# Half of a mixture-of-experts gate table summed in HBM by indirect DMAs, the other half by one-hot products among 56 expert inputs

## Chip, core and metric

The kernel runs on one core of one Trainium2 chip. Its metric is the device time of one execution in microseconds; less is better.

## What is computed

Two transformer-like blocks over 256 tokens of width 1024, in f32. The change is in the last part, a retrieval from 128 x 128 = 16,384 experts ("PEER"). Cut to what matters:

```python
q = (x @ peer_w_q).reshape(n_tok, 8, 2, 128)            # 8 heads, two halves
s = einsum('thcd,hckd->thck', q, sub_keys)              # scores of 2 x 128 sub-keys
v_top, i_top = lax.top_k(s, 16)
cand = v_top[:, :, 0, :, None] + v_top[:, :, 1, None, :]
best, pos = lax.top_k(cand, 16)                         # 16 of 256 pairs, for each head
expert = i_top_0 * 128 + i_top_1                        # at pos
gate = softmax(best)
act = gelu(einsum('tkd,td->tk', u_emb[expert], x)) * gate
out = einsum('tk,tkd->td', act, v_emb[expert])          # 8 x 16 experts a token
```

## The kernel before, in words

The kernel does not gather experts. It computes the inputs u.x of all 16,384 experts for all tokens, multiplies them by a dense gate table, and sums the outputs. Experts are taken in 128 groups of 128: group e holds the experts whose second sub-key is e, with the first sub-key on the partitions. So the work of group e is one **input** product ("up": 128 experts x 256 tokens, over 8 tiles of the width), a Gelu on ScalarE, three operations on VectorE that multiply by the gates and split the result into a high and a low part (`gate`), and one **output** product ("down": 256 tokens x 1024, over the 128 experts, accumulated in four PSUM banks until the end).

**Weights.** SyncE streams pages of 1 MB (two pieces of 128 x 1024) from `in_stream` into a ring of three. A page is sent when the pieces of the page three before it have been taken. A piece is used in one of two ways: *whole* (f32, straight from the ring; `whole`), or *split*: ScalarE writes its high part to one of three `piece` buffers (`high`, line 1217), VectorE the low part (`low`, line 1730), and PE makes three products of high and low parts (`fm_piece`, `down`). ScalarE may write a piece when PE has begun the piece two before it.

**Selection.** VectorE finds the best pairs head by head (`select`). For each head it makes a one-hot of the places in the lists (line 2381), GpSimd numbers them (`number`, lines 425 and 431), and one head later VectorE sums the result into `selv` (`gather`, line 2389; the last head's in line 2472): row number, column number and gate of each token's 128 experts.

**The gate table.** `selv` is transposed (line 1116), so that for each token the 128 chosen experts lie on the partitions. Then for each token VectorE (line 2483, and line 2480 for four tokens at a time) and ScalarE (lines 1655 and 1661, every other four tokens) write a one-hot of the row numbers and a one-hot of the column numbers times the gates; PE multiplies the two (a product of 128 x 128 x 128), and ScalarE copies four tokens at a time to the table `G` (line 1646), which takes the whole arena, 128 KB of each partition.

**Order.** The query products, then nine whole inputs under the selection, the transposes, a tenth input, the 256 tokens of one-hot products with the whole inputs 10 to 13 put between them, step by step, one split input (14), 13 outputs, then rounds of one output and one input (113 of them, groups of six in a loop), two outputs, and the final norm. The inputs that run ahead are kept in `early`, 15 tiles of 128 x 256.

**Other places that the change touches.** In the FFN of the first block GpSimd does two multiplications for each of 22 page turns (`gated_page`, lines 389 and 392). Between 50 and 157 us it issues 16 plain DMAs of 1 MB (line 370) for modulation weights. `acc_free`, `acc_ready`, `a_ready`, `lo_ready`, `piece_used` are semaphores, named for what they count. `SCRATCH` is the memory for GpSimd's DMA descriptors. All matrix products are recorded at line 462 (the transposes of `selv` at 1116).

Of the kernel before, what the change touches and what calls it, by code (L numbers as in the profile page):

```python
# [14 lines left out]
P = 128  # L15
D = 1024
KD = D // P
L = 256
RING = 3
LOOP = 6  # L20
EARLY = 15
CHOICE = 10
SCRATCH = 1024
F32 = mybir.dt.float32
# [10 lines left out]
         ("gt", 8), ("pm", 2), ("pr", 2), ("w2", 4), ("wq", 8), ("early", EARLY // 2), ("first", (EARLY - 1) // 2),  # L35
         ("peer", 129 - EARLY)]
# [10 lines left out]
NWHOLE = PAGE["first"] - WHOLE0  # L47
# [13 lines left out]
for _name, _n in TURNS:  # L61
# [7 lines left out]
        ("if_b", 2), ("eps6", 1), ("eps_gn", 1), ("eps_ml", 1)]  # L69
# [14 lines left out]
def widths(table):  # L84
# [14 lines left out]
 p1_mm mt_ready places place_no placed hi_ready g_mm selt_sb piece_used acc_ready hn_mm hn_sq hn_sqmm  # L99
# [3 lines left out]
 p1_sb x_mm xa_mm lv_sb u0_mm xa_sb s_sb sa_mm sa_sb ds_mm u0_sb y_mm y_sb xs_root x_in_psum subk_in key_sb  # L103
 key_mm selt_ready selt_mm oh_ready row_hot g_sb a_ready experts_done ach hn_cs hn_ln hn_root xfin c_in cols_in
 lg_ready root1 hraw h_hi wctx_arg wctx w_q part_hi decay_arg conv_mid conv_u mqk_conv lf_abs lf_ln mqk_taps
 m_arg m_exp zs_ready kk_root scan_done g_arg g_exp row_square fg_in fin_sq fin_root dch h_new part_in up_chain
# [3 lines left out]
def build(nc, t, out):  # L110
    with ExitStack() as ctx:
# [13 lines left out]
        early = place("early", SPARE, [EARLY, L])  # L125
# [36 lines left out]
        def pair(name, hi, lo, a):  # L162
# [110 lines left out]
        eqb = at(19456, 2048)  # L273
        selv = at(21504, 768).rearrange("p (t c n) -> p t c n", t=2, c=3)
        gsm = at(22272, 64)
        subk = at(28672, 2048).rearrange("p (g n) -> p g n", g=16)
        G = arena[:, 0:32768].rearrange("p (n e) -> p n e", e=128)
        selT = at(0, 768, late).rearrange("p (c n) -> p c n", c=3)

        row_hot = [v.rearrange("p (n e) -> p n e", n=4) for v in (at(768, 512, late), at(1280, 512, late), row_more, small)]  # L280
        up_bank = (TURN["peer"] + EARLY - 1) % 2
        gate_banks = (6, 7, 1 - up_bank)
        col_hot = [v.rearrange("p (n e) -> p n e", n=2) for v in (at(1792, 256, late), cols[:, 0:256],
                                                                  pc[:, 0:256])]
        col_hot = [[v[:, 0], v[:, 1]] for v in col_hot] + [[cols[:, 256:384], pc[:, 256:384]]]
        gelu_t = at(0, 512, late).rearrange("p (b n) -> p b n", b=2)
        a_r = late_r[:, 768:1792].rearrange("p (c b n) -> p c b n", c=2, b=2)
# [29 lines left out]
        def _(sp):  # L317
# [35 lines left out]
            pages_split(PAGE["first"] + RING, NPAGES - PAGE["first"] - RING, 2 * (WHOLE0 - SPLIT0))  # L353


# [9 lines left out]
        def _(pool):  # L365
# [27 lines left out]

            with pool.Fori(0, 3) as i:
                for u in range(LOOP):
                    gated_page(u, i)
            for u in range(18, 22):
                gated_page(u)
# [35 lines left out]
            for hh in range(7):  # L434
                number(hh)

            first = PAGE["first"]
            for s in range(2):
                c = piece_no(first) + s
                if s == 0:  # L440
                    pool.wait_ge(loaded[first % RING], 16 * (first // RING + 1))
                pool.wait_ge(S["piece_used"], c - 1 - s)
                g.tensor_copy(piece[:, 0, c % 3], ring[:, first % RING, s]).then_inc(S["hi_ready"], 1)
# [3 lines left out]
        def _(pe):  # L447
# [25 lines left out]
            def turn(T, i=0):  # L473

                v = T // 2 + LOOP // 2 * i
                if not (isinstance(v, int) and v <= 0):
                    pe.wait_ge(acc_free[T % 2], v)
# [624 lines left out]
            m.then_inc(S["x_in_psum"], 1)  # L1102
# [5 lines left out]

            for e in range(CHOICE - 1):
                early_up(e)  # L1110
            pe.wait_ge(S["key_sb"], 8)
            for tt in range(2):
                pe.wait_ge(S["selt_ready"], tt + 1)
                pe.wait_ge(S["placed"], 8)
                for c in range(3):
                    m = nc.tensor.transpose(ps[:, 6 + tt, c * P:(c + 1) * P], selv[:, tt, c, :], ident)
                m.then_inc(S["selt_mm"], 1)
            early_up(CHOICE - 1)


            def scatter(q):
                for b in range(2):
                    pe.wait_ge(S["oh_ready"], 2 * q + b + 1)
                    if b == 0:
                        if q % 2 == 1:
                            pe.wait_ge(S["row_hot"], q // 2 + 1)
                        if q >= 3:
                            pe.wait_ge(S["g_sb"], q - 2)
                    for e in range(2):
                        c = 2 * b + e  # L1130
                        m = mm(ps[:, gate_banks[q % 3], c * P:(c + 1) * P], row_hot[q % 4][:, c, :],
                               col_hot[2 * (q % 2) + b][e], start=True, stop=True)
                    m.then_inc(S["g_mm"], 1)

            def early_step(n):
                e, k = CHOICE + n // 8, n % 8
                T, p = TURN["peer"] + e, PAGE["early"] + e // 2
                if k == 0:
                    turn(T)
                    turn(T + 1)  # L1140
# [1542 lines left out]
```

## Time and profile before

| | us |
|---|---|
| device time, median of 3 runs | 1698.72 (1697.33 to 1699.45) |
| profiled execution, span | 1701.3 (its device time is not given apart from the span) |
| PE busy in it | 1646.9 (97%) |
| VectorE, ScalarE, GpSimd busy | 1174.0, 801.9, 99.0 |
| DMA | 278.94 MB, mean 164 GB/s |

The profile is of one more execution. In it, L462 is line 462 of the kernel; PE is TensorE's matmul, PEld its weight load, DVE VectorE, ACT ScalarE, POOL GpSimd, SP SyncE; a q behind an engine's name is its instruction queue. An f32 product leaves two records, a product of split parts one. Matmuls overlap, and their ends are modelled: a group's length is a little more than the time to the start of the next, so steps are best read from starts.

### The profile page before, as it was taken

Reading aid. Unit: us, or ns where it says so; the run is one execution under the profiler, and the core shown is the slowest. Engines: PE = TensorE matmul, PEld = TensorE weight load, DVE = VectorE, ACT = ScalarE, POOL = GpSimd, SP = SyncE. Lnnn points to the kernel's source line nnn. Section 1 sums busy time; section 2 is a strip of 40 time slices with the busy share of each in tenths; the row PEclk is TensorE's granted clock in tenths of the full one; section 3 lists DMA queues with packets and bytes.
Section 4 is the critical chain, followed back from the end, with each engine's and each line's share of the span. In section 5 each row is a group of like instructions: output and inputs, shape, how many; then the busy total and the mean of one; then the engine's idle time right before and its main releaser. Section 6 shows DMA issues by size and latency. Waiting matters only on the chain.

```text
span 1701.3 us, 32624 instructions
## 1 busy us (share of the span) xinstructions
PE 1646.9 (97%) x12606; PEld 1510.4 (89%) x12606; DVE 1174.0 (69%) x2143; ACT 801.9 (47%) x1223; POOL 99.0 (6%) x124
## 2 busy tenths in 40 slices
PE   8999999999999999989999989999999999999998
PEld 3999978999999998879898878999999999999997
DVE  3756656777846769647498998666666666666665
ACT  2423436566634675425213993444444444444444
POOL 0000000022200001110052000000000000000000
PEclk9999999999999999999999999999999999999999
DMA  8876414545554433204333015555555555455553
GB/s 307 303 272 223 149 50 149 189 175 191 179 176 149 152 144 125 101 4 158 115 124 124 26 50 187 185 195 176 196 178 192 185 185 193 177 197 176 194 183 126
DMA packets 38826, 278.94 MB, mean 164 GB/s; under 512 B 4432, under 2 KB 4560, under 8 KB 5328
## 3 DMA queue, kind: packets, MB, share of 16 engines
q1 hardware_dynamic: 35424, 254.82, 42.1%
q0 software_dynamic: 2304, 16.78, 2.6%
q10 hardware_dynamic: 1008, 6.05, 0.9%
q8 instruction: 68, 1.11, 0.3%
q14 instruction: 22, 0.18, 0.0%
HBM read 276.58 MB, written 1.05 MB: 163 GB/s over the span
## 4 chain that ended last, share of the span: by engine, by line
PE 86%; DVE 7%; ACT 4%; issue 2%; DMA 1%; DVEq 0%; POOL 0%; SPq 0%; ACTq 0%; POOLq 0%
PE ps L462 86%; DVE piece L1730 2%; DMA ring<-in_stream 1%; ACT piece L1217 1%; DVE pconst_sb L2483 1%; DVE cols L2483 0%; DMA arena<-in_xT 0%; DVE late L2483 0%; DVE arena L1780 0%; ACT arena L1256 0%; DVE arena L1833 0%; DVEq L2483 0%; ACT arena L1575 0%; ACT L1252 0%; DVE arena L1797 0%
## 5 line engine op out<-in xcount | busy, mean ns | idle before, releaser
L462 PEld LDWEIGHTS ps<-h_r,piece 128*128 128x128 f32 x5664 | 699.2, 192 | 19.8 <-issue 8.7
L462 PE MATMUL ps<-h_r,piece 128*128 128x256 f32 x5664 | 708.4, 284 | 4.6 <-DVE piece L1730 3.7
L1730 DVE TENSOR_TENSOR piece<-ring,piece 128x1024 fp32r<-128x1024 f32 x434 | 533.2, 1237 | 241.7 <-ACT piece L1217 240.3
L1217 ACT ACTIVATE piece<-ring 128x1024 fp32r<-128x1024 f32 x432 | 452.6, 1056 | 356.8 <-PE ps L462 352.7
L462 PE MATMUL ps<-piece,late_r 128*128 128x512 f32 x1536 | 370.1, 391 | 1.4 <-DVE late_r L2505 1.4
L462 PEld LDWEIGHTS ps<-piece,late_r 128*128 128x128 f32 x1536 | 281.1, 188 | 55.3 <-issue 1.8
L2500 DVE TENSOR_TENSOR late<-late,arena 128x256 f32<-128x256 f32 x113 | 72.0, 638 | 117.6 <-ACT late L1686 117.6
L1686 ACT ACTIVATE late<-ps 128x256 f32<-128x256 f32 x113 | 43.5, 385 | 200.5 <-PE ps L462 200.5
L462 PE MATMUL ps<-arena,ring 128*128 128x256 f32 x480 | 110.5, 379 | 1.6 <-DVE arena L1797 1.6
L462 PEld LDWEIGHTS ps<-arena,ring 128*128 128x128 f32 x480 | 88.1, 190 | 12.3 <-issue 2.0
L462 PE MATMUL ps<-arena 64*64 64x64 f32 (+7 forms) x930 | 87.4, 297 | 7.6 <-DVE arena L2266 1.8
L462 PEld LDWEIGHTS ps<-arena 64*64 64x64 f32 (+4 forms) x930 | 68.6, 162 | 22.1 <-issue 10.4
L1244 ACT ACTIVATE arena<-ps 128x512 f32<-128x512 f32 x43 | 25.6, 595 | 97.0 <-PE ps L462 97.0
L462 PE MATMUL ps<-ffn_hi,piece 128*128 128x256 f32 x352 | 63.5, 283 | 1.2 <-DVE piece L1730 1.2
L2505 DVE TENSOR_TENSOR late_r<-late,late_r 128x256 fp32r<-128x256 f32 x128 | 54.5, 426 | 4.4
L462 PEld LDWEIGHTS ps<-ffn_hi,piece 128*128 128x128 f32 x352 | 54.9, 192 | 1.4 <-DVE piece L1730 1.4
L462 PE MATMUL ps<-ffn_lo,piece 128*128 128x256 f32 x176 | 49.8, 283 | 0.0
L462 PE MATMUL ps<-mg_hi,piece 128*128 128x256 f32 x256 | 42.8, 284 | 0.5 <-DVE arena L1995 0.5
L2503 DVE CAST late_r<-late 128x256 fp32r<-128x256 f32 x128 | 37.7, 294 | 4.4
L462 PE MATMUL ps<-piece,h_r 128*128 128x256 f32 x288 | 38.9, 297 | 0.0
L462 PEld LDWEIGHTS ps<-mg_hi,piece 128*128 128x128 f32 x256 | 37.7, 192 | 0.9 <-DVE arena L1995 0.9
L462 PEld LDWEIGHTS ps<-piece,h_r 128*128 128x128 f32 x288 | 37.8, 205 | 0.8 <-issue 0.8
(325 smaller groups left out, 1709.5 us busy)
## 6 DMA issues: line engine op xcount, KB each, us to landing
ring<-in_stream SPq DMA_DIRECT2D x240, 1024.0 KB, 4.8
arena<-in_mod POOLq DMA_DIRECT2D x16, 1024.0 KB, 6.2
arena<-in_const ACTq DMA_DIRECT2D x1, 2256.0 KB, 10.6
arena<-in_const ACTq DMA_DIRECT2D x1, 1648.0 KB, 8.8
xres<-in_xT SPq DMA_DIRECT2D x1, 1024.0 KB, 5.3
arena<-in_xT SPq DMA_DIRECT2D x1, 1024.0 KB, 7.1
arena<-in_subk ACTq DMA_DIRECT2D x1, 1024.0 KB, 4.9
out<-arena SPq DMA_DIRECT2D x4, 256.0 KB, 2.1
```

What stands on the lines that cost most here:

```text
L462: mm_last[0] = nc.tensor.matmul(*args, **kw)
L1217: A(piece[:, 0, c % 3], ring[:, p % RING, s], ACT.Copy).then_inc(S["hi_ready"], 1)
L1244: A(dst, ps[:, T % 2, src], func, **kw).then_inc(acc_free[T % 2], 1)
L1686: A(gelu_t[:, e % 2, :], ps[:, T % 2, 0:L], ACT.Gelu).then_inc(acc_free[T % 2], 1)
L1730: TT(piece[:, 1, c % 3], ring[:, p % RING, s], piece[:, 0, c % 3].bitcast(F32), ALU.subtract).then_inc(S["lo_ready"], 1)
L2483: ins = TS(col_hot[b % 4][e], iota, selT[:, 1, bass.ds(16 * i + (2 * b + e), 1)], selT[:, 2, bass.ds(16 * i + (2 * b + e), 1)], ALU.is_equ ...
L2500: TT(a_t, ready, G[:, :, bass.ds(LOOP * i + e, 1)].rearrange("p n a -> p (n a)"), ALU.mult).then_inc(S["a_chain"], 1)
L2503: V.tensor_copy(a_r[:, 0, b, :], a_t).then_inc(S["a_chain"], 1)
L2505: TT(a_r[:, 1, b, :], a_t, a_r[:, 0, b, :].bitcast(F32), ALU.subtract).then_inc(S["a_ready"], 1)
```

## The change

Tokens 0 to 127 and tokens 128 to 255 get their gates in different ways.

- **Tokens 0 to 127**: the table is an HBM tensor `gate_table` of 128 x 128 x 128. GpSimd writes zeros to it with eight DMAs of 1 MB, issued during the FFN (from a tile `zero`). As each head is selected, VectorE works out its gates (`gate_arg` to `gate_end`, with one small Exp of ScalarE for each head, `gate_exp`) and its positions `gidx` (expert x 128 + token). GpSimd adds each of the 16 columns of a head to the table with an indirect DMA (one element for each of 128 tokens, `compute_op=add`): four after each numbering of heads 1 to 6, the other 104 after it. Before the first DMA of a head it waits for those of the head before. SyncE waits for all 128, then fetches the table back, two expert groups at a time, into three tiles `gtile`, between the pages.
- **Tokens 128 to 255**: one transposition, one-hots on VectorE alone, and one-hot products in groups of four tokens (`quad`) behind two of each three split inputs. The table `G` for them takes 64 KB of each partition, laid out with tokens innermost.
- **Order**: 16 whole inputs, 2 split inputs, three transposes, 54 split inputs with 32 groups of four tokens among them, 56 rounds of one output and one input, 72 outputs. So 72 inputs run ahead of the first output; they are kept in the arena and in `early` (now 12 tiles). The pages of the stream are in that order.
- **Gates** are now two multiplications of 128 x 128, one from `gtile` and one from `G`, then the cast and the subtraction as before, in a ring of three buffers instead of two.

```diff
-EARLY = 15
-CHOICE = 10
-SCRATCH = 1024
+CHUNK = 4
+EARLY = 16
+AHEAD = 72
+SCRATCH = 4096
...
+            for p in range(UPS + RING, PEER + 2):
+                next_page(p)
+            sp.wait_ge(S["scat"], 2048)
+            for m in range(RING):
+                gate_in(m)
+            m = RING
+            for n in range(2, P - AHEAD // 2):
+                next_page(PEER + n)
+                if n > P - AHEAD or (n < P - AHEAD and n >= 2 * m - 1):
+                    gate_in(m)
+                    m += 1
...
+            def gate_in(m):
+
+                if m >= RING:
+                    sp.wait_ge(S["a_ready"], 2 * (m - RING) + 2)
+                sp.dma_start(gtile[:, m % RING], gate_pair[m]).then_inc(g_in[m % RING], 16)
...
+            g.memset(zero, 0.0).then_inc(S["mqk_pad"], 1)
...
                     gated_page(u, i)
+                    if u % 3 == 0:
+                        pool.dma_start(gate_zero[u // 3 + 2 * i], zero).then_inc(S["zeroed"], 16)
+            for n in range(6, 8):
+                pool.dma_start(gate_zero[n], zero).then_inc(S["zeroed"], 16)
...
+            def scatter(first, last):
+                for n in range(first, last):
+                    hh, k = n // 16, n % 16
+                    if k == 0:
+                        pool.wait_ge(S["gate_at"], 2 * hh + 2)
+                        if hh:
+                            pool.wait_ge(S["scat"], 256 * hh)
+                    g.indirect_dma_start(gtab[:, :], bass.IndirectOffsetOnAxis(ap=gidx[:, hh, k:k + 1], axis=0),
+                                         gw[:, hh, k:k + 1], None, compute_op=ALU.add).then_inc(S["scat"], 16)
+
+            number(0)
+            for hh in range(1, 7):
                 number(hh)
+                scatter(CHUNK * (hh - 1), CHUNK * hh)
+            scatter(6 * CHUNK, 128)
...
+            def quad(q, i=0):
+                pe.wait_ge(S["oh_ready"], q + 1 + 8 * i)
+                if not isinstance(i, int) or q >= 2:
+                    pe.wait_ge(S["g_sb"], q + 8 * i)
+                for n in range(4):
+                    m = mm(ps[:, 6 + q % 2, n * P:(n + 1) * P], row_hot[q % 2][:, n, :], col_hot[q % 2][:, n, :], start=True,
+                           stop=True)
+                m.then_inc(S["g_mm"], 1)
...
+            with pe.Fori(1, 4) as i:
+                for n in range(2 * LOOP):
+                    up(EARLY + 8 + n, C0 + 8 + n, i)
+                    if n % 3 < 2:
+                        quad(2 * (n // 3) + n % 3, i)
+            def both(k, i=0):
+                down(k, C1 + 2 * k, i)
+                up(AHEAD + k, C1 + 2 * k + 1, i)
...
+            for e in range(EARLY - 2):
+                gelu(e)
+                if e in (1, 4, 7, 11):
+                    gate_exp(4 + (1, 4, 7, 11).index(e))
...
+                if n >= 8 and (n - 8) % 3 < 2:
+                    q = 2 * ((n - 8) // 3) + (n - 8) % 3
+                    act.wait_ge(S["g_mm"], q + 2)
+                    A(G[:, :, 4 * q:4 * q + 4].rearrange("p e n -> p n e"),
+                      ps[:, 6 + q % 2, :].rearrange("p (n e) -> p n e", n=4), ACT.Copy).then_inc(S["g_sb"], 1)
...
+            def gate_end(hh):
+
+                after(roots[hh])
+                for tt in range(2):
+                    ins = TT((gw[:, hh], wsel(hh)[:, 1])[tt], wsel(hh)[:, tt],
+                             gsm[:, 2 * hh + tt:2 * hh + tt + 1].to_broadcast([P, 16]), ALU.mult)
+                ins.then_inc(S["gate_at"], 1)
+                after(nos[hh])
+                TS(gidx[:, hh, :], no_t, 128.0, col("tok"), ALU.mult, ALU.add).then_inc(S["gate_at"], 1)
...
+            def onehots(q):
+                r, c = row_hot[q % 2], col_hot[q % 2]
+                if q >= 2:
+                    dve.wait_ge(S["g_mm"], q)
+                TT(r, iota.unsqueeze(1).to_broadcast([P, 4, P]),
+                   selT[:, 0, 4 * q:4 * q + 4].unsqueeze(2).to_broadcast([P, 4, P]), ALU.is_equal)
+                for n in range(4):
+                    ins = TS(c[:, n, :], iota, selT[:, 1, 4 * q + n:4 * q + n + 1], selT[:, 2, 4 * q + n:4 * q + n + 1],
+                             ALU.is_equal, ALU.mult)
+                ins.then_inc(S["oh_ready"], 1)
...
+            def gate(e):
+                m, b = e // 2, e % 3
+                z, a_t = gtile[:, m % RING, e % 2, :], z_of(e)
+                if e % 2 == 0:
+                    dve.wait_ge(g_in[m % RING], 16 * (m // RING + 1))
+                if e >= 3:
+                    d = e - 2
+                    dve.wait_ge(S["piece_used"], piece_no(PEER) + (2 * d if d < P - AHEAD else P - AHEAD + d) + 1)
+                elif e == 0:
+                    dve.wait_ge(S["g_sb"], 33)
+                    dve.wait_ge(acc_free[(TURN["peer"] + AHEAD - 1) % 2], (TURN["peer"] + AHEAD - 1) // 2 + 1)
+                TT(a_t[:, 0:P], a_t[:, 0:P], z, ALU.mult).then_inc(S["a_chain"], 1)
+                TT(a_t[:, P:L], a_t[:, P:L], G[:, e, :], ALU.mult).then_inc(S["a_chain"], 1)
...
+            for k in range(P - AHEAD):
+                low(PEER + k, 0)
+                gate(k)
+                low(PEER + k, 1)
+            for n in range(P - AHEAD, P - AHEAD // 2):
+                for s in range(2):
+                    low(PEER + n, s)
+                    gate(2 * n - (P - AHEAD) + s)
```

## Rows read from the trace of the kernel before

**Rows 1.** The page, chain of work that ended last: share of the span by engine.

```profile
PE 86%; DVE 7%; ACT 4%; issue 2%; DMA 1%; DVEq 0%; POOL 0%; SPq 0%; ACTq 0%; POOLq 0%
```

**Rows 2.** Stretches: from:to, length, busy us (instructions) of each engine, PEclk, DMA share, GB/s.

```profile
921.00:1014.00 93.00, 80.99 (x595) 73.60 (x596) 88.88 (x290) 88.47 (x230) 2.02 (x2) 1.00 0.10 35
1057.00:1690.00 633.00, 632.84 (x4058) 577.64 (x4058) 420.72 (x563) 271.08 (x338) 0.00 (x0) 1.00 0.52 184
```

**Rows 3.** Timeline of PE: start, length, line, tiles, number of records, [idle before].

```profile
888.52 31.25 PE L462 MATMUL ps<-arena,ring 128*128 128x256 f32 x144
920.98 0.85 PE L1116 MATMUL ps<-pconst_sb,arena 128*128 128x128 f32 x6 [1.22 <-DVE arena L2472]
...
925.95 0.68 PE L462 MATMUL ps<-late 128*128 128x128 f32 x4 [0.68 <-ACT early L1244]
...
934.95 0.61 PE L462 MATMUL ps<-late,row_more 128*128 128x128 f32 x4
...
935.85 0.60 PE L462 MATMUL ps<-arena,ring 128*128 128x256 f32 x2
...
1014.35 3.11 PE L462 MATMUL ps<-h_r,piece 128*128 128x256 f32 x24
...
1021.58 35.62 PE L462 MATMUL ps<-piece,late_r 128*128 128x512 f32 x156 [1.38 <-DVE late_r L2505]
1057.37 3.14 PE L462 MATMUL ps<-h_r,piece 128*128 128x256 f32 x24 [0.16 <-DVE piece L1730]
...
1689.79 5.63 PE L462 MATMUL ps<-piece,late_r 128*128 128x512 f32 x24
```

**Rows 4.** Timeline of ScalarE and VectorE behind one input of the loop.

```profile
1060.63 0.39 ACT L1686 ACTIVATE late<-ps 128x256 f32<-128x256 f32 x1 [1.78 <-PE ps L462]
1060.91 1.05 ACT L1217 ACTIVATE piece<-ring 128x1024 fp32r<-128x1024 f32 x1
1061.17 0.63 DVE L2500 TENSOR_TENSOR late<-late,arena 128x256 f32<-128x256 f32 x1 [1.06 <-ACT late L1686]
...
1062.17 0.43 DVE L2505 TENSOR_TENSOR late_r<-late,late_r 128x256 fp32r<-128x256 f32 x1
```

**Rows 5.** Timeline of VectorE in the one-hot stretch.

```profile
936.18 0.68 DVE L2480 TENSOR_TENSOR late<-pconst_sb,late 128x512 f32<-128x512 f32 x1
936.78 0.60 DVE L2483 TENSOR_SCALAR late<-pconst_sb,late 128x128 f32<-128x128 f32 x2
```

**Rows 6.** Timeline of VectorE in the selection of the last two heads.

```profile
904.20 1.23 DVE L2381 TENSOR_TENSOR arena<-pconst_sb,arena 128x1024 f32<-128x1024 f32 x1
...
911.91 0.26 DVE L2389 TENSOR_TENSOR arena<-arena 128x64 f32<-128x64 f32 x1
...
913.75 1.23 DVE L2381 TENSOR_TENSOR arena<-pconst_sb,arena 128x1024 f32<-128x1024 f32 x1
```

**Rows 7.** Timeline of ScalarE, between two early Gelus.

```profile
916.75 1.28 ACT L1634 ACT_TABLE_LOAD   x1
```

**Rows 8.** The stretch in which GpSimd's plain DMAs run; columns as in rows 2.

```profile
50.00:160.00 110.00, 109.14 (x922) 108.46 (x922) 74.21 (x68) 41.87 (x60) 8.66 (x16) 0.98 0.76 284
```

**Rows 9.** Timeline of all engines where GpSimd issues one of them.

```profile
75.07 1.22 DVE L1730 TENSOR_TENSOR piece<-ring,piece 128x1024 fp32r<-128x1024 f32 x1
...
75.45 0.53 POOL L370 DMA_DIRECT2D arena<-in_mod  x1 [1.93 <-DVE arena L1885]
```

**Rows 10.** DMA issues: number, KB each, median us from issue to landing.

```profile
ring<-in_stream SPq DMA_DIRECT2D x240, 1024.0 KB, 4.8
...
out<-arena SPq DMA_DIRECT2D x4, 256.0 KB, 2.1
```

**Rows 11.** Timeline of GpSimd: the end of the last numbering.

```profile
908.08 2.68 POOL L431 TENSOR_TENSOR arena<-arena 128x512 f32<-128x512 f32 x3
```

**Rows 12.** Timeline of GpSimd and VectorE, where GpSimd casts.

```profile
930.49 2.02 POOL L443 CAST piece<-ring 128x1024 fp32r<-128x1024 f32 x2 [19.73 <-DMA ring<-in_stream]
930.53 2.06 DVE L2483 TENSOR_SCALAR cols<-pconst_sb,late 128x128 f32<-128x128 f32 x2
```

More of the change, by code:

```diff
@@ L280, in build @@
[L280 to L285, printed above, removed]
@@ L1118, in _ @@
[L1118 to L1133, printed above, removed]
@@ L1199, in _ @@
+            C2 = C1 + P - AHEAD
+            with pe.Fori(0, 5) as i:
+                for e in range(P - AHEAD, P - AHEAD + 2 * LOOP):
+                    down(e, C2 + e, i, 2 * LOOP)
+            for e in range(P - AHEAD + 10 * LOOP, P):
+                down(e, C2 + e)
         @block.scalar
@@ L1624, in _ @@
                     key_evac(u - 1)
+                if u in (3, 4, 6, 7):
+                    gate_exp((3, 4, 6, 7).index(u))
             key_evac(7)
[L1627 to L1634 removed]
@@ L1692, in _, with gelu @@
-            split(PAGE["peer"])
-            rounds = (P - EARLY) // LOOP
-            with act.Fori(0, rounds) as i:
-                for u in range(LOOP):
-                    split(PAGE["peer"] + 1 + u, i)
-                    gelu(EARLY + u, i)
-            for u in range(LOOP * rounds, P - EARLY):
-                split(PAGE["peer"] + 1 + u)
-                gelu(EARLY + u)
+            def gelu(e):
+                if e >= AHEAD:
+                    act.wait_ge(S["a_ready"], e - AHEAD + 1)
+                evac(TURN["peer"] + e, z_of(e), ACT.Gelu, slice(0, L))
@@ L1701, in _ @@
+            for k in range(P - AHEAD):
+                split(PEER + 1 + k)
+                gelu(AHEAD + k)
+            for n in range(P - AHEAD + 1, P - AHEAD // 2):
+                split(PEER + n)
             act.wait_ge(S["a_ready"], P)
@@ L2512, in _ @@
-            for e in range(EARLY - 2):
-                early_gate(e)
-                if e < EARLY - 3:
-                    low(PAGE["first"] + (e + 2) // 2, (e + 2) % 2)
-            low(PAGE["peer"], 0)
-            early_gate(EARLY - 2)
-            early_gate(EARLY - 1)
-            low(PAGE["peer"], 1)
-            rounds = (P - EARLY) // LOOP
-            with dve.Fori(0, rounds) as i:
-                for u in range(LOOP):
-                    split(PAGE["peer"] + 1 + u, i)
-                    gate(EARLY + u, i, gelu_t[:, (EARLY + u) % 2, :])
@@ L2525, in _ @@
-            for u in range(LOOP * rounds, P - EARLY):
-                split(PAGE["peer"] + 1 + u)
-                gate(EARLY + u, 0, gelu_t[:, (EARLY + u) % 2, :])
+            for k in range(P - AHEAD):
+                low(PEER + k, 0)
[5 more added lines that the diff above has]
+                    gate(2 * n - (P - AHEAD) + s)
             dve.wait_ge(S["fg_in"], 16)
```

304 lines of the change are left out of this document (125 added, 179 removed).

## Prediction

> **What bounds the kernel now.** I read the page first: PE is busy for most of the span, and 86% of the chain that ended last is its matmuls [rows 1]. Since a busy PE need not be at its best rate, the second view is the table of stretches around the change [rows 2]. The reader is to see two kinds there: the one-hot stretch (921 to 1014), where VectorE and ScalarE are busier than PE and DMA all but rests at 35 GB/s, and the expert rounds (from 1057), where PE has no free time in 633 us and VectorE has a third of it. The third view is PE's timeline, which gives the step of each kind of product by the starts of neighbouring groups [rows 3]:
> - a whole f32 expert input: nine (144 records) take 31.25 us: 3.47.
> - one expert output ("down"): 13 lie between 1021.58 and 1057.37: 35.79 / 13 = 2.753 us.
> - one output and one split input: 113 rounds lie between 1054.62 (1057.37 less one output) and 1689.79: 5.621 us. So a split input takes 2.868 us.
> - one token's one-hot product: four tokens between 934.95 and 935.85: 0.225 us each.
> - the end: the last two outputs start at 1689.79 and end in step at 1695.3; 6.0 us of final norm follow.
>
> The one-hot stretch from 925.95 to 1014.35 lasts 88.4 us: 256 x 0.225 = 57.6 us of one-hot products, 4 x 3.47 = 13.9 us of expert inputs put between them, and 16.9 us of waits for one-hot rows. That, with the waits beside it, is what can be gained; everything else in the expert phase is products that stay.
>
> **The sum, along PE's queue.** Nothing before 888.5 is on it (below). From there:
> - 16 whole inputs (before: 14): 55.5, to 944.0.
> - 56 split inputs: 160.6. Three transposes instead of six (which took 0.85 at 920.98): 0.4. 128 tokens of one-hot products: 28.8. To 1133.8.
> - The first output waits: gate(0) now waits for the evacuation of input 71, the last before it. In the loop of before the input ends in step at 1060.24, ScalarE's Gelu runs from 1060.63 to 1061.02, VectorE's chain from 1061.17 to 1062.60 [rows 4]. The strided multiply (0.63) gives way to two contiguous ones over half as many elements, 0.2 each, so the chain is 1.2: 0.4 + 0.4 + 0.15 + 1.2 = 2.2 us, to 1136.0.
> - 56 rounds of output and input: 314.8. 72 outputs: 198.2. Tail 6.0. End: 1655.0.
>
> That is 46.3 us under the profiled span of 1701.3, which is 2.6 us above the median of the runs shown. The forecast is 1698.7 - 46.3 = 1652 us. From the other side: gone are 128 tokens (28.8), the waits of the stretch (16.9) and around it (1.22 at 920.98, 0.68 at 925.95, 0.16 at 1057.37, and 1.5 at 1021.58, which starts 7.23 us after 1014.35 where an input and an output take 5.62), and 0.4 of transposes; added are the slower form of two inputs (1.2) and the new wait (2.2): -46.3.
>
> **What has to stay hidden.** *VectorE and ScalarE in the 56 inputs.* Three inputs and two groups of four tokens take PE 3 x 2.868 + 2 x 0.90 = 10.4 us. VectorE then does three low parts (1.22 each [rows 9]) and two sets of one-hots: a row multiply (step 0.60) and four comparisons (0.60 for two, 0.34 for one: step 0.26) [rows 5], 3.7 + 3.3 = 7.0 us. ScalarE does three high parts (1.05), three Gelus (0.39) [rows 4] and two evacuations of twice a Gelu's elements (0.6, or 1.2 if the strided write doubles it): 5.6 to 6.8 us. Both fit. If each of the 32 groups still caught PE out by the 0.16 us of 1057.37, that is +5; I take none.
> *VectorE in the 72 outputs alone.* The 13 outputs before 1057 are this pattern (low part, multiply, cast, subtraction), and PE doesn't wait among them. The multiply gets cheaper; the tiles' arrival is rival 3.
> *Selection on VectorE.* Seven small operations a head (0.1 to 0.2 each), less those for all heads at the end: some 5 us. The places of the last head are summed at 926 instead of at 920.98 less a little [rows 3]. PE asks for them only after 18 inputs, at 949.7, and for the first low part at 944.0. Each of the last four Exp costs ScalarE a table load before it and one after it (1.28 [rows 7]); with a Gelu that is some 3.2 us inside a step of 3.47. Head 7's values are found near 918 (911.9 now [rows 6]), ScalarE comes to its Exp at 930. Nothing on the path.
> *GpSimd's zeroing.* Eight writes of 1 MB each during the FFN, one to three pages of 5.74 us (two split inputs' products each). Nearest row: between 50 and 160 us 16 DMAs of GpSimd run beside the stream at 284 GB/s, and PE is busy for 109.1 of 110 us [rows 8]. A page that lands in 4.8 us [rows 10] has some 9 us from issue to use (two pages less 2.5 for its parts). I take 0; 8 x 1 us would be the cost if that cover were short.
>
> **The indirect DMAs, the unknown price.** GpSimd issues 128, each for 128 single elements; call its time for one X. Below: 0.53 us, a plain DMA of 128 rows from GpSimd [rows 9]. Above: 2.1 us, the landing of the one kind of DMA into HBM here [rows 10], as if each ran alone. It must read an index for each row and add to HBM, so it lies off the lower end, but nothing makes it wait for a landing within a head: I take 1.3. 24 are issued between heads, four after each numbering. Numbering ends at 910.76 [rows 11], 5.3 us after VectorE's one-hot of the places (904.20 to 905.4), and is wanted at 911.9, with 9.55 us from head to head [rows 6]. Four at 1.3 are 5.2 us; free are 9.55 - 5.3 + 0.7 (the new operations) + 1.1 = 6.1, so selection isn't held up. The other 104 start at 915 and, with six waits for a head's landing at 2.1, end at 915 + 104 X + 12.6: at 983, 1063 or 1146 for X = 0.53, 1.3, 2.1. SyncE waits for them, with the pages of expert pair 2 and after, and VectorE's first gate tile, queued behind: due at about 1128. At my value 65 us are left.
>
> **Rivals.**
> *1. The table is late.* From X = 1.93 each further 0.1 us costs 10.4 us; at X = 2.37 the gain is gone. At the upper bound of 2.1 the time is 1670. Against it: a plain issue takes a quarter of that. For it: no row shows an adding DMA of single elements, and if the DMA engines take each addition as a round trip, X is theirs, not GpSimd's.
> *2. GpSimd locks VectorE out: slower.* At 930.49 GpSimd runs two casts in 2.02 us; the two comparisons that VectorE starts at 930.53 take 2.06 together instead of 0.60: one comparison gets through per GpSimd instruction [rows 12]. If an indirect DMA does the same, then per three inputs VectorE needs 3.7 + 1.2 + 8 x (0.34 + X) = 18.0 us at X = 1.3 where PE needs 10.4, for as long as the scattering lasts. It also stretches selection (up to four waits in each of six heads, 31 us: PE stands still from 944 for 14), so the last 104 start at 947; some 79 are left at the first one-hots, 12 go per three inputs: 6.6 x 7.6 = 50 us. The time is 1652 + 14 + 50 = 1716. It decides against the change from X = 1.15 on; at X = 1.0 the same sum gives 1689. Against it: at 75.45 GpSimd issues a plain DMA amid VectorE's low part, and that takes 1.22 us, the DMA 0.53, as each does alone [rows 9]. But that is a subtraction of two operands; no row has a comparison or a cast beside a DMA issue.
> The Trainium skill (SBUF — State Buffer, "Who interferes with whom") says that GpSimd and a VectorE scalar operation or copy in its two-port mode take one shared pair of ports as an exclusive lock for the whole instruction, and that generating descriptors needs that pair. The casts beside the comparisons agree; by the whole rule this rival, and not the forecast, would hold.
> *3. Gate tiles hold up the stream.* In the 72 outputs SyncE waits for a gate before it sends the next tile, the next page behind it. If page and tile went one after the other (4.8 + 2.1 us [rows 10]), two outputs would take 6.9 instead of 5.5: 36 x 1.4 = 50 us, no change. Against it: three pages are in flight, and the traffic, 1.18 MB in 5.5 us or 214 GB/s, is under the 284 of [rows 8].
>
> **How the numbers follow.** Forecast 0.70. Rival 1 0.11, of which 0.05 still faster (1655 to 1695) and 0.06 slower. Rival 2 0.14: 0.06 in part or with a short X (1655 to 1690), 0.08 slower. Rival 3 0.03, the same. Others 0.02. Faster 0.81, the same 0.04, slower 0.15, where 0.2% is about what a measurement can tell from no change. The forecast's own range is 1647 (all of the new wait and of the two inputs' 1.2 hidden, one-hots 2 us cheaper in bulk) to 1660 (+5 at the groups, +3 of zeroing). With the faster halves of rivals 1 and 2 the range is 1642 to 1690.
>
> **What would show it.** Right: split inputs from about 944, the first output at about 1136, outputs alone from about 1451, PE without idle time in each; comparisons at 0.34; GpSimd's last indirect DMA well before 1128. Wrong: comparisons of 1 us and more with PE waiting for them (rival 2); a gap of PE at 1136 released by a DMA, with SyncE waiting for the scatter (rival 1); PE waiting for pages or tiles after 1451 (rival 3). What makes the forecast wrong is above all X over 1.93, or a lock with X over 1.15.

## The result and the profile after

| | before | after |
|---|---|---|
| median | 1699.1 us (4 runs, 1697.3 to 1700.1) | 1709.3 us (4 runs, 1706.4 to 1711.8) |
| span of the profiled execution | 1701.3 us | 1710.1 us |
| ratio of the times | | 1.0059, 95% interval 1.0043 to 1.0074 |

The change makes the kernel slower by 0.6%. 1652 was forecast.

The first view to read is the table of stretches: the one in which inputs and one-hot products run together, and the one after it (columns as in rows 2).

```profile
1000.00:1100.00 100.00, 79.28 (x629) 76.44 (x628) 48.52 (x91) 42.93 (x58) 71.54 (x42) 0.98 0.47 114
1210.00:1504.00 294.00, 294.00 (x1884) 268.19 (x1883) 185.93 (x313) 125.72 (x158) 0.00 (x0) 1.00 0.56 198
```

In the rounds PE is busy for 294.00 of 294.00 us, as before [rows 2]. Amid the one-hots it is busy for 79 of 100, and there no other engine is full: VectorE has 49, ScalarE 43, GpSimd 72. So nobody lacks capacity; somebody waits in the wrong order. PE's timeline shows where (start, length, line, tiles, number of records, [idle before]):

```profile
886.90 55.42 PE L512 MATMUL ps<-arena,ring 128*128 128x256 f32 x256
941.97 6.10 PE L512 MATMUL ps<-h_r,piece 128*128 128x256 f32 x48
...
1140.72 1.16 PE L512 MATMUL ps<-late 128*128 128x128 f32 x8 [1.58 <-DVE late L2507]
1141.63 3.11 PE L512 MATMUL ps<-h_r,piece 128*128 128x256 f32 x24
1146.03 1.16 PE L512 MATMUL ps<-row_more,late 128*128 128x128 f32 x8 [1.28 <-DVE row_more L2507]
1146.94 5.99 PE L512 MATMUL ps<-h_r,piece 128*128 128x256 f32 x48
1154.22 1.16 PE L512 MATMUL ps<-late 128*128 128x128 f32 x8 [1.28 <-DVE late L2507]
...
1193.44 2.97 PE L512 MATMUL ps<-piece,late_r 128*128 128x512 f32 x12 [1.98 <-DVE late_r L2537]
```

The whole inputs take the 55 us of the sum, and the split inputs start at 941.97 where 944 was said. The reader is then to see the brackets: every group of four tokens (x8) finds PE idle for 1.3 us and more, until VectorE's comparisons (L2507) are done. Three inputs and two groups take 1154.22 - 1140.72 = 13.5 us where the sum had 10.4. The first output starts at 1193.44, 57.4 us behind the 1136.0 of the sum. From there to the end of the span are 516.7 us; the sum had 519.0. All of the error lies between 942 and 1193.

What VectorE and ScalarE did around one such group, in their timelines, with PE's in the same stretch:

```profile
1055.25 1.16 PE L512 MATMUL ps<-late 128*128 128x128 f32 x8 [1.43 <-DVE late L2507]
1056.17 3.10 PE L512 MATMUL ps<-h_r,piece 128*128 128x256 f32 x24
1060.56 1.16 PE L512 MATMUL ps<-row_more,late 128*128 128x128 f32 x8 [1.29 <-DVE row_more L2507]
```

```profile
1056.57 1.06 ACT L1249 ACTIVATE piece<-ring 128x1024 fp32r<-128x1024 f32 x1 [4.26 <-PE ps L512]
1057.53 0.36 ACT L1276 ACTIVATE arena<-ps 128x256 f32<-128x256 f32 x1
1057.79 1.11 ACT L1688 ACTIVATE arena<-ps 128x512 f32<-128x512 f32 x1
```

```profile
1057.66 1.22 DVE L1724 TENSOR_TENSOR piece<-ring,piece 128x1024 fp32r<-128x1024 f32 x1 [2.46 <-ACT piece L1249]
1058.80 0.68 DVE L2504 TENSOR_TENSOR late<-pconst_sb,late 128x512 f32<-128x512 f32 x1
1059.40 1.11 DVE L2507 TENSOR_SCALAR row_more<-pconst_sb,late 128x128 f32<-128x128 f32 x4
```

This is a ring of waits. PE begins an input at 1056.17; only then is a slot in the ring of three pieces free, and ScalarE makes the high part of the input two further on (1056.57 to 1057.63). VectorE waited 2.46 us for it, since that input's low part stands in its queue ahead of the one-hots (low part to 1058.88, one-hots to 1060.51). PE, done with its input, waits for these one-hots at 1060.56. From the start of an input to the one-hots behind it pass 4.39 us of other engines' serial work, though PE needs 2.87; the difference comes back at every group. The one-hots themselves had all their data the whole time.

The second view is the source line of the indirect DMAs (times in ns min/median/max; first and last start), and the source line of the comparisons.

```profile
L486 POOL DMA_INDIRECT gate_table<-early x128: 1548/1561/2601, 862.4 to 1183.7; - x128
its engine sat idle before it (us, times) until:
  issue: 69.1, 123
  DMA gate_table<-early: 11.2, 5
```

```profile
L2507 DVE TENSOR_SCALAR late<-pconst_sb,late x64: 333/342/659, 968.8 to 1183.3; 128x128 f32<-128x128 f32 x64
L2507 DVE TENSOR_SCALAR row_more<-pconst_sb,late x64: 335/340/559, 974.1 to 1184.9; 128x128 f32<-128x128 f32 x64
...
  PE ps L512: 46.5, 31
```

A comparison takes 0.34 us with indirect DMAs beside it most of the time, as it does alone [rows 5]. The median indirect DMA takes 1.56 us, with 0.30 before the next: 1.86, above the 1.3 taken. The last one starts at 1183.7; in the sum it was issued by 1063. Around the first output:

```profile
1187.35 1.41 SPq L379 DMA_DIRECT2D early<-gate_table  x3
...
1191.50 0.38 ACT L1276 ACTIVATE early<-ps 128x256 f32<-128x256 f32 x1 [0.43 <-PE ps L512]
1192.01 0.29 DVE L2532 TENSOR_TENSOR arena<-arena,early 128x128 f32<-128x128 f32 x1 [3.93 <-ACT early L1276]
```

The gate tiles are asked for at 1187.35, and VectorE's first gate multiply still waits for the Gelu, not for them. So the table came just in time, for a first output that was 57 us late for another reason. Each of the two delays, that of the inputs (57 us) and that of the table (due at about 1128, asked for at 1187), is longer than the 46 us that were to be gained, and the profile shows only the one that ended last.

### The profile page after: what moved, and what is told of

Same layout as the page of the kernel before. It is cut to its first block, busy times and chain, and to the rows that moved or that the text cites. A ratio compares the mean times of both kernels' runs of the same rounds, so it can differ in the third digit from the quotient of the medians.

```text
span 1710.1 us, 30322 instructions
## 1 busy us (share of the span) xinstructions
PE 1625.2 (95%) x12331; PEld 1489.3 (87%) x12331; DVE 1129.1 (66%) x2190; ACT 754.0 (44%) x1042; POOL 319.9 (19%) x259
## 4 chain that ended last, share of the span: by engine, by line
PE 80%; DVE 10%; ACT 5%; DMA 2%; issue 2%; DVEq 0%; POOL 0%; SPq 0%; POOLq 0%
PE ps L512 80%; DVE piece L1724 4%; ACT piece L1249 3%; DVE late L2504 1%; DVE late L2507 1%; DVE row_more L2507 1%; DMA ring<-in_stream 1%; DMA arena<-in_const 1%; DMA arena<-in_xT 0%; DVE arena L1774 0%; ACT arena L1288 0%; DVE arena L1827 0%; ACT arena L1607 0%; ACT L1284 0%; DVE arena L1791 0%
## 5 line engine op out<-in xcount | busy, mean ns | idle before, releaser
L512 PEld LDWEIGHTS ps<-h_r,piece 128*128 128x128 f32 x5616 | 692.6, 193 | 15.3 <-issue 9.2
L512 PE MATMUL ps<-piece,late_r 128*128 128x512 f32 x1536 | 359.0, 390 | 2.0 <-DVE late_r L2537 2.0
L486 POOL DMA_INDIRECT gate_table<-early x128 | 217.0, 1695 | 80.2 <-issue 69.1
L1276 ACT ACTIVATE arena<-ps 128x256 f32<-128x256 f32 (+1 forms) x163 | 71.3, 437 | 256.6 <-PE ps L512 256.6
L512 PEld LDWEIGHTS ps<-arena,ring 128*128 128x128 f32 x512 | 96.7, 190 | 14.8 <-issue 2.0
L512 PEld LDWEIGHTS ps<-arena 64*64 64x64 f32 (+4 forms) x930 | 70.3, 169 | 22.0 <-issue 10.4
L426 POOL TENSOR_TENSOR arena<-arena 128x256 f32<-128x256 f32 x22 | 16.2, 737 | 211.4 <-DVE arena L2049 211.4
L2537 DVE TENSOR_TENSOR late_r<-arena,late_r 128x256 fp32r<-128x256 f32 x120 | 51.1, 426 | 4.1
L1688 ACT ACTIVATE arena<-ps 128x512 f32<-128x512 f32 x32 | 35.2, 1101 | 33.0 <-PE ps L512 30.9
L512 PE MATMUL ps<-row_more,late 128*128 128x128 f32 x128 | 18.9, 291 | 24.7 <-DVE row_more L2507 24.7
L470 POOL TENSOR_TENSOR arena<-arena 128x512 f32<-128x512 f32 x14 | 20.4, 1686 | 116.3 <-DVE arena L2375 116.3
```

The costliest lines, as they stand in the source:

```text
L426: g.tensor_tensor(v, ga[:, b, :], v, ALU.mult).then_inc(S["gated"], 1)
L470: g.tensor_tensor(e[:, 2 * c:2 * c + 2], e[:, 2 * c:2 * c + 2], topf[:, :, 2 * hh + c, :].unsqueeze(2).to_broadcast([P, 2, 16, 16]), ALU.m ...
L486: g.indirect_dma_start(gtab[:, :], bass.IndirectOffsetOnAxis(ap=gidx[:, hh, k:k + 1], axis=0), gw[:, hh, k:k + 1], None, compute_op=ALU.ad ...
L512: mm_last[0] = nc.tensor.matmul(*args, **kw)
L1276: A(dst, ps[:, T % 2, src], func, **kw).then_inc(acc_free[T % 2], 1)
L1688: A(G[:, :, 4 * q:4 * q + 4].rearrange("p e n -> p n e"), ps[:, 6 + q % 2, :].rearrange("p (n e) -> p n e", n=4), ACT.Copy).then_inc(S["g_ ...
```

## The experiments

**1. One-hots one input earlier.** VectorE's queue alone is changed:

```diff
-            for n in range(NU + 2):
+            for n in range(NU + 1):
                 if n < NU:
                     low(UPS + n // 2, n % 2)
-                p = n - 2
+                p = n - 1
```

> The changed kernel with one edit: VectorE makes the one-hots for the group behind input p after the low part of piece p+1 instead of p+2. Theory A (VectorE's queue order: the low part of piece p+2 can't start before PE has begun input p, and the one-hots stand behind it): PE's 46.5 us of waits for one-hots nearly all go (under 5 us left) and the split inputs end near 1145 instead of 1191. But GpSimd's last indirect DMA still ends near 1185, so the first output still starts at about 1193 and the time stays within 5 us of 1709: the wait moves to the table. Theory B (GpSimd's DMA issue locks VectorE's comparisons out, my rival 2): the waits for one-hots stay above 35 us.

Measured: 1723.1 us, ratio 1.0136 (1.0116 to 1.0156). PE's timeline of this kernel:

```profile
1124.55 3.11 PE L512 MATMUL ps<-h_r,piece 128*128 128x256 f32 x24
1203.57 4.68 PE L512 MATMUL ps<-piece,late_r 128*128 128x512 f32 x12 [75.91 <-DVE late_r L2537]
```

No group waits any more and the inputs end at 1127.7. The order was the cause of the 46.5 us. But PE then stands still for 75.9 us, until the table is there: the wait has moved, and grown. The time is 14 us above the changed kernel's, where at most 5 were expected. The last indirect DMA starts at 1197.0, 13 us later than in the changed kernel, though the 25th started 5 us sooner: long DMAs cost 9.5 us more and gaps over 0.6 us 8.5 us more.

**2. and 3. No indirect DMAs**, in the changed kernel and in the one of experiment 1 (both leave out the gates of tokens 0 to 127):

```diff
-                    g.indirect_dma_start(gtab[:, :], ..., gw[:, hh, k:k + 1], None, compute_op=ALU.add).then_inc(S["scat"], 16)
+                    g.engine_nop().then_inc(S["scat"], 16)
```

> The changed kernel without the 128 indirect DMAs (the gates of tokens 0 to 127 stay zero, the semaphore is counted up by empty instructions), the order of VectorE as it is. Theory A: the waits for one-hots stay (over 35 us), since they have nothing to do with GpSimd; selection ends some 10 us earlier, off the path; time 1700 to 1710. Theory B: the waits go, time about 1655.

> Both edits: one-hots one input earlier, and no indirect DMAs (gates of tokens 0 to 127 stay zero). Theory A: PE runs through the split inputs, first output near 1137, time 1652 to 1660, the sum of the prediction. Theory B gives the same; what would speak against both is a time above 1670.

Measured: 1708.6 us (ratio 1.0063, 1.0040 to 1.0086) with the one-hots where the change has them, 1651.0 us (ratio 0.9716, 0.9699 to 0.9733) with the one-hots early. Without a single indirect DMA the groups' waits are the same 46.4 us (24.7 + 21.7), so GpSimd has no part in them. With both obstacles away the sum of the prediction holds to a microsecond:

```profile
1125.28 1.06 PE L511 MATMUL ps<-late 128*128 128x128 f32 x8
...
1129.04 1.06 PE L511 MATMUL ps<-row_more,late 128*128 128x128 f32 x8
1129.86 3.11 PE L511 MATMUL ps<-h_r,piece 128*128 128x256 f32 x24
1134.95 2.99 PE L511 MATMUL ps<-piece,late_r 128*128 128x512 f32 x12 [1.98 <-DVE late_r L2536]
```

The four corners (1709.3, 1723.1, 1708.6, 1651.0) are to be read together: taking away either cause alone gives nothing or loses 14 us, taking away both gives 58.

**4. A quarter of the room for descriptors:** `SCRATCH = 1024` in the changed kernel, the value of before.

> The changed kernel with a quarter of the memory for GpSimd's DMA descriptors (1024 instead of 4096). GpSimd stands idle for 45 us in 16 gaps of 1.7 to 6 us between indirect DMAs. If it waits there for room for descriptors, the gaps get longer and more (over 80 us), and the last DMA ends after 1220, time over 1740. If the gaps have another cause (a fetch of instructions, a wait for the DMA engines that carry pages), they stay at 35 to 55 us and the time at 1709.

Measured: 1802.2 us (one run); over 1740 was expected if the gaps are waits for room.

```profile
L486 POOL DMA_INDIRECT gate_table<-early x128: 1548/1565/2498, 865.2 to 1275.1; - x128
its engine sat idle before it (us, times) until:
  issue: 153.6, 122
```

The DMAs themselves are as short as before, but the idle time ahead of them grows from 69.1 to 153.6 us, in gaps of 1.7 to 5.7 us after one to three DMAs. Part of the gaps is a wait for room. Counting the DMAs shows which: with 1,024 bytes the gaps over 1.6 us stand behind each 3rd and each 7th DMA, and with 4,096 bytes, in the changed kernel, behind each 15th and each 28th. Some are hidden by a numbering or by the wait at a head's end.

**5. Half the rows in each indirect DMA**, one-hots early: `gidx[0:64, ...]`, `gw[0:64, ...]`. The gates of tokens 64 to 127 are left out.

> One-hots one input earlier, and each indirect DMA takes the gates of tokens 0 to 63 alone (64 rows in place of 128; the gates of tokens 64 to 127 are left out). Theory A (the price of an indirect DMA goes with its rows, and so does the room that its descriptors take): one takes about 0.8 us in place of 1.56, no gaps beside the waits between heads, the table is done before the last input ahead, the first output's product starts near 1135 and the time is that of the kernel without scatter, 1651, within 4 us. Theory B (a fixed price for each DMA): one still takes about 1.56 us and 1.86 with its gap, only the gaps for room go: last DMA at about 928 + 104 x 1.86 + 11 (between heads) = 1132 to 1150, first output near 1140 to 1158, time 1657 to 1675.

Measured: 1681.2 us (ratio 0.9901, 0.9873 to 0.9929), above both ranges.

```profile
L486 POOL DMA_INDIRECT gate_table<-early x128: 1408/1416/3066, 859.7 to 1154.3; - x128
```

Half the rows take 1.416 us in place of 1.56: a straight line through the two gives an estimate of some 1.27 us fixed and 2.3 ns for each row. Theory A falls. The gaps over 0.6 us sum to 34 us against 53 in experiment 1, so those for room don't all go, as theory B had it, and the table is late by 31.2 us of PE's time. The gaps now stand behind each 28th and each 51st DMA: one count goes by rows (15 to 51), the other doesn't.

**6. to 8. Room, with a control.** One-hots early; 68 inputs ahead in place of 72, and three buffers of earlier stages elsewhere, leave 8,192 bytes. The control is the same kernel with 4,096; the third has `CHUNK = 5`.

```diff
-AHEAD = 72
-SCRATCH = 4096
+AHEAD = 68
+SCRATCH = 8192
```

> One-hots one input earlier, 8,192 bytes of descriptor room in place of 4,096; the room comes from 68 expert inputs ahead in place of 72 (the table is then due 11.5 us earlier) and from buffers of an earlier stage put elsewhere. Nothing is left out. Theory A (the gaps that are not at a head's end are waits for room): some 34 us of gaps go, the last indirect DMA is issued at 928 + 104 x 1.86 + 11 (between heads) + 0 to 17 (lengthened ones) = 1132 to 1150, first output near 1157 against 1124 due, time 1651 + 33 = 1684 (1672 to 1694), so below the kernel before. Theory B (the gaps come from the DMA engines being shared with the weights and stay whatever the room): last DMA near 1190, time 1651 + 75 = 1726 or more.

> The same kernel as the one with 8,192 bytes of room, with 4,096 again (68 ahead, all else the same): the control. Both theories: the last indirect DMA as late as with one-hots early and 72 ahead, 1197, first output near 1203, and as the inputs end 11.5 us earlier the wait is 87 us and the time 1723 + 11 = 1734 (1726 to 1740).

> 8,192 bytes of room, one-hots early, 68 ahead, and five indirect DMAs behind each head's numbering in place of four, so that 98 in place of 104 are left behind the last. Theory A (GpSimd has that much time between the heads: 6.2 us of numbering and 5 x 1.86 = 15.5 us against a period of 12.6, so it hasn't): the heads' period grows toward 15.5 and the selection becomes later, the time is 0 to 20 us above that of four. Theory B (selection has slack before TensorE needs it): 6 DMAs earlier, 11 us less than with four.

Measured: 1725.7 (ratio 1.0153, 1.0129 to 1.0178), 1732.0 (1.0196, 1.0158 to 1.0234) and 1721.8 us (1.0123, 1.0097 to 1.0149). First 8,192, then 4,096 bytes:

```profile
L486 POOL DMA_INDIRECT gate_table<-early x128: 1548/1557/3037, 861.3 to 1185.9; - x128
its engine sat idle before it (us, times) until:
  issue: 53.5, 123
```

```profile
L486 POOL DMA_INDIRECT gate_table<-early x128: 1547/1559/3318, 860.2 to 1193.3; - x128
its engine sat idle before it (us, times) until:
  issue: 68.0, 123
```

Doubling the room takes 14.5 us from the idle time put down to "issue" and brings the last DMA 7.4 us forward, the time down by some 6. Theory A said that 34 us go: it was right in kind and far off in size, and the time is the one that theory B gave. The gaps for room stand behind each 30th and each 56th DMA now, and from the 25th DMA on they sum to 15.8 us in place of 30.2: doubling the room halves them. Of the 53.5 us that stay, 37 are the 123 steps of 0.30. The fifth DMA per head gained 4 us at most between two kernels whose runs overlap (1723.0 to 1726.9 and 1717.3 to 1729.0), and its last DMA started later (1190.9); nothing is to be had there.

**9. and 10. Other comparisons.** In the traces with early one-hots DMAs of 2.0 to 3.3 us stand beside the one-hots. The four TENSOR_SCALAR of a group were replaced:

```diff
-                for n in range(4):
-                    ins = TS(c[:, n, :], iota, selT[:, 1, 4 * q + n:4 * q + n + 1], selT[:, 2, 4 * q + n:4 * q + n + 1],
-                             ALU.is_equal, ALU.mult)
+                made = dn(TT(c, iota.unsqueeze(1).to_broadcast([P, 4, P]), spread[1], ALU.is_equal))
...
+                after(made)
+                TT(c, c, spread[2], ALU.mult).then_inc(S["oh_ready"], 1)
```

> One-hots one input earlier, 4,096 bytes, 72 ahead, and the column one-hots made by two TENSOR_TENSOR instructions of 128x512 (compare, then multiply by the gates) in place of four TENSOR_SCALAR of 128x128. Nothing is left out. Theory A (VectorE's TENSOR_SCALAR comparisons hold GpSimd's indirect DMAs up, not the other way round: the DMAs of 2.3 to 3.0 us are those that run beside them, and none is over 2 us once the one-hots have ended): the long DMAs go, some 25 us of their time with them, the last is issued near 1172 in place of 1197, the first output's product starts near 1178 against 1203.6, and the time is 1723 - 25 = 1698 (1690 to 1704). Theory B (the long ones come from the DMA queues): last DMA near 1197, 1723 within 4.

> The same with five indirect DMAs behind each head's numbering in place of four. With 8,192 bytes five gave 4 us less than four. Theory A (the DMAs set the end, so 6 of them earlier are 11 us less, and the heads' period grows from 12.6 to 14.5, which gives some of it back): 3 to 8 us less than the kernel with four, so near 1692 (1685 to 1700). Theory B (the DMAs don't set the end any more): the same time as with four.

Measured: 1721.4 (ratio 1.0122, 1.0105 to 1.0139) and 1725.1 us (1.0150, 1.0136 to 1.0163). In the second the last DMA starts at 1201.3, so the fifth one behind each head gained nothing. Theory A falls in the form it was given: the last DMA starts at 1194.0 in place of 1197.0, and what the DMAs from the 25th on take above 1.56 us sums to 20.8 us in place of 24.9. The time is the one that theory B gave, but its reason isn't borne out either. The DMAs' source line in the kernel of experiment 1, first in the stretch of the one-hots, then in the 66 us in which GpSimd alone works on:

```profile
L486 POOL DMA_INDIRECT gate_table<-early x65: 1550/1569/3333, 947.1 to 1124.6; - x65
```

```profile
L486 POOL DMA_INDIRECT gate_table<-early x32: 1549/1554/1573, 1130.2 to 1195.2; - x32
```

With VectorE and ScalarE idle and no page moving, 32 of 32 take 1.55 to 1.57; beside them they take up to 3.33. With comparisons as TENSOR_TENSOR the longest is 2.65. So something that runs in that stretch holds GpSimd up whichever form the comparisons have. These two rows don't tell VectorE from ScalarE and the pages, since all three stop together. The timeline of experiment 1 does, when each DMA is laid beside what VectorE is doing as it starts:

```profile
1063.56 1.23 DVE L1724 TENSOR_TENSOR piece<-ring,piece 128x1024 fp32r<-128x1024 f32 x1 [1.75 <-ACT piece L1249]
1063.94 2.30 POOL L486 DMA_INDIRECT gate_table<-early  x1 [0.30 <-issue]
...
1066.55 1.56 POOL L486 DMA_INDIRECT gate_table<-early  x1 [0.30 <-issue]
1066.58 1.23 DVE L1724 TENSOR_TENSOR piece<-ring,piece 128x1024 fp32r<-128x1024 f32 x1 [0.17 <-ACT piece L1249]
...
1068.33 1.23 DVE L2507 TENSOR_SCALAR row_more<-pconst_sb,late 128x128 f32<-128x128 f32 x4
1068.41 1.55 POOL L486 DMA_INDIRECT gate_table<-early  x1 [0.30 <-issue]
```

The first DMA starts while VectorE is in a low part (a TENSOR_TENSOR) with 0.85 us to go, and takes 0.74 us more than 1.56. The second starts just before a low part and the third amid comparisons: both take their 1.55. So it goes all through: from the 25th DMA on, 31 of 104 start while a TENSOR_TENSOR runs, and they hold 23.0 of the 24.9 us; the rest is one DMA of 3.33 us that starts 0.08 us before a low part. In the changed kernel it is 42 DMAs and 15.3 of 15.4 us, with TENSOR_TENSOR comparisons 51 DMAs and 20.7 of 20.8. In the same stretch 24 DMAs start while ScalarE works and no TENSOR_TENSOR runs; above 1.555 us they take 0.12 us in all 24 together, with pages moving. That is read from the times of the traces; no run moved the low parts themselves.

**11. and 12. Fewer heads scattered**, one-hots early: the last call is `scatter(6 * CHUNK, 64)` and `scatter(6 * CHUNK, 96)`, and SyncE waits for that many.

> One-hots one input earlier and indirect DMAs for heads 0 to 3 alone, 64 in place of 128 (the gates of heads 4 to 7 of tokens 0 to 127 are left out). Theory A (what costs in the whole kernel with early one-hots is only that the table is late; the DMAs that run beside the inputs take nothing from TensorE): the 64th was issued at 1049 with all 128, so the table is ready long before 1128, the first output's product starts near 1135 and the time is that without scatter, 1651 within 3 us. Theory B (the DMAs or their traffic also slow the inputs or the 56 rounds): 1655 or more with the table in time.

> The same with heads 0 to 5, 96 indirect DMAs (the gates of heads 6 and 7 of tokens 0 to 127 are left out). Theory A: with all 128 the 96th was issued at 1134, so it lands near 1139 and the gate tiles near 1143; the first output's product starts near 1144, 9 us behind 1135: 1660 (1655 to 1666). Each further DMA then costs about 2 us: 32 of them bring the 1723 of all eight heads. Theory B: more than 1666.

Measured: 1653.7 (ratio 0.9725, 0.9700 to 0.9749) and 1653.9 us (0.9727, 0.9705 to 0.9749), the second below the 1655 to 1666 that were expected. Both leave out the gates of the heads that aren't scattered. PE's timeline with six heads:

```profile
1133.82 5.46 PE L512 MATMUL ps<-piece,late_r 128*128 128x512 f32 x12 [3.66 <-DVE late_r L2537]
```

With 96 indirect DMAs (the last at 1127.1, 7 us sooner than the 96th of 128 in experiment 1) the wait is 3.66 us, of which 1.98 is there without any. Scattering beside the inputs costs PE 3 us at most. The 32 DMAs more of experiment 1 cost 1723.1 - 1653.9 = 69 us: 2.2 us each, all of it lateness.

## Why the prediction was wrong

Point by point, by its own steps.

- *The sum along PE's queue* was right: whole inputs 55 us, split inputs 2.87, rounds 5.62, 72 outputs without a wait, new wait 1.98 (2.2 taken). A group with the input behind it takes 3.76 us in experiment 3, less 2.87 that is 0.22 for each of four tokens (0.225 taken). It gives 1652; experiment 3 gave 1651.0.
- *"Both fit. If each of the 32 groups still caught PE out by the 0.16 us of 1057.37, that is +5; I take none."* This is the step that failed. It compared busy time per three inputs (7.0 against 10.4 us, and that was right: VectorE is half idle), and never laid the operations out in queue order. The order in the code, low part of input p + 2 ahead of the one-hots behind input p, with three pieces, makes a serial path of 4.39 us per input. Cost: 46.5 us of waits in 31 groups. Each wait costs a further 0.27: a group with its input takes 5.31 us (1140.72 to 1146.03) with an idle time of 1.28 in it, where experiment 3 has 3.76 (1125.28 to 1129.04) without; 5.31 - 1.28 - 3.76 = 0.27, 8 us in 31 groups. And PE's granted clock, 1.00 in this stretch of experiment 3, drops three times for a few us amid the waits; two inputs then take 7.4 us in place of 6.0, 4 us in all:

```profile
991.00:998.00 7.00, 6.98 (x48) 6.77 (x47) 2.72 (x3) 3.66 (x5) 4.48 (x4) 0.80 0.57 154
```

  Together 58.5; less the 1.6 us by which the whole inputs start sooner that is 56.9 of the 57.4 found.
- *ScalarE's strided evacuation* took 1.10 us, the upper of the two values named (0.6 or 1.2). Where it stands ahead of a high part the group's wait is 2.06 and not 1.28.
- *Selection, the table loads, zeroing* were hidden, as said: the whole inputs start at 886.90, 1.6 us sooner than before [rows 3], and PE asks for the head's values without waiting. The 1.6 us are no gain: in experiments 1 to 3, the same up to there but for the indirect DMAs, they start at 882.28, 883.91 and 887.59. But four DMAs at 1.86 don't fit between the numberings: the heads' period on GpSimd is 12.6 us, not 9.55, and the 25th DMA starts at 936.9, not 915.
- *X* was mis-sized: 1.3 taken, 1.86 measured. The last DMA ended at 1185.6 and not at 1063: 22 us by the later start, 58 by 104 x 0.56, 15.4 by DMAs longer than 1.56, some 27 by gaps above the 0.30 and the 12.6 us allowed for heads. In the prediction's formula (915 + 104 X + 12.6) an end at 1185.6 is X = 2.48, beyond the 2.37 at which rival 1 said that the gain is gone; experiment 1 shows this rival alone. One DMA with the 0.30 behind it, 1.86, is within the upper bound of 2.1; what the bound left out are the waits for room, which no row of before could show and the constant `SCRATCH` in the diff hinted at, and the DMAs lengthened by VectorE.
- *Rival 2* is refuted in its direction: comparisons take 0.34 us beside the DMAs, at most 0.66 (0.35 in experiment 2, without DMAs), and the low part that starts inside a DMA at 1066.58 takes its 1.23. It is the other way round: GpSimd is the one that is held up, by 15 us in the changed kernel and 25 with early one-hots. The Trainium skill (SBUF — State Buffer, "Who interferes with whom") has the whichever-issues-first rule, by which both directions are possible, and says that a GpSimd DMA seen stalled by VectorE is starved while making descriptors; it infers that TENSOR_TENSOR doesn't starve it. Of the first rule the traces bear out one direction alone: a DMA that starts amid a TENSOR_TENSOR is held for about what that has left. The inference doesn't agree with them: the DMAs held up are those that start amid a TENSOR_TENSOR, and no DMA that starts amid comparisons in TENSOR_SCALAR form was long, but for the 3.33 us one with the low part right behind.
- *Rival 3* didn't occur: no wait in the outputs.
- *The stated range* of 1642 to 1690 has a lower end for which no term of the sum stands; the forecast's own began at 1647.

The two failures hid each other. The change alone shows 46.5 us of waits for comparisons and a table in time; a reader who mended only that would have lost 14 us more. No version with all its gates beat the kernel before: with early one-hots the table would have to be some 25 us sooner.

What stays open: whether the DMAs would keep to 1.56 us if the low parts were moved, which only the times of the traces say; and what the two counts behind the waits for room stand for, of which one changes with the rows of a DMA.

## What to carry to other kernels

Before a stretch is called covered, lay out each engine's queue for one period, with who releases what: an operation whose inputs have long been ready still waits for everything queued ahead of it, and a buffer ring closes that into a loop. When a trace shows a wait, ask what would end last without it (here a table that came just in time), and test the repair together with the removal of the next limit. For a resource that no row shows, such as room for descriptors, bound the effective price over many operations, not that of one.

## What the runs showed of the hardware

- An indirect DMA that adds 128 single f32 elements in HBM holds GpSimd for 1.56 us, one with 64 for 1.42, with 0.30 us to the next; so most of it is fixed.
- One that starts while VectorE is in a TENSOR_TENSOR takes longer by about the time that this has left, less 0.12 us: within 0.06 us in 47 of 51 cases of the changed kernel and 32 of 40 of experiment 1. The longest, of 3.03 us, exceed that by 0.6; why isn't shown.
- The room for descriptors sets gaps: GpSimd's idle time put down to issue for 128 DMAs was 153.6 us with 1,024 bytes and 69.1 with 4,096 in the changed kernel, 68.0 with 4,096 and 53.5 with 8,192 in experiments 7 and 6. The gaps stood behind each 3rd and 7th, 15th and 28th, 30th and 56th DMA.
- After 76 us without work PE's first output takes 4.68 us in place of 2.97; the granted clock in the gap is the lower level, 1.2 GHz (first row). So long a gap isn't needed: in experiment 12 PE waits 3.66 us, the first output takes 5.46, and the clock is at the lower level too (second row). In experiment 3 it waits 1.98 us, and the output takes 2.99 at 2.4 GHz.

```profile
1150.00:1200.00 50.00, 0.00 (x0) 0.00 (x0) 0.00 (x0) 0.00 (x0) 36.07 (x24) 0.50 0.21 0
1133.00:1139.00 6.00, 5.18 (x12) 4.13 (x13) 4.12 (x8) 1.06 (x1) 0.00 (x0) 0.50 0.96 350
```
